# Normalising each head pair inside the scan stage, with the first pair's inverse made one stage earlier

## The chip, the cores and the metric

The kernel runs on one core of a Trainium2 chip. Five engines work side by side, each through its own instructions in program order: TensorE (PE) for matrix products, VectorE (DVE), ScalarE (ACT) and GpSimd (POOL) for work on rows, and SyncE (SP), which here issues most of the DMAs. They meet by semaphores. The metric is the device time of one launch in microseconds (us), lower is better.

## The reference, cut to what matters

The program is two whole network blocks. The change touches one layer of the second, an RWKV-7 mixer with 16 heads of width 64 over 768 positions (512 latent, 256 context), scanned in both directions:

```
r, k, v, z, decays, a, kk = features(h)            # 1024 channels = 16 heads x 64
state_t = state_(t-1) * decay_t + (rank-one corrections from kk, a, k, v)
y_t     = state_t r_t,  forward and backward, summed
y       = (y - mean(y over the head)) * rsqrt(var(y over the head) + 64e-5) * ln_gain + ln_bias
y       = (y + bonus) * gate          # bonus = (sum_head r*kd*r_k) * v, gate from z
x       = x + layer_gate * (y @ w_out)
```

The scan is done in chunks of 64 positions. Each chunk needs the inverse of a unit lower triangular matrix; it is built from the inverses of its 32x32 diagonal blocks, and these come from forward substitution.

## The kernel before

The program is a list of stages. Between stages every compute engine waits until all four have finished the last one (`stage_done`, in `program`, L3126 in the profile is that wait's drain); SP only waits where a stage's `sync` says so. For the RWKV layer the stages are norm, `RwkvFeatures`, `RwkvTerms`, `RwkvScan`, `RwkvOutput` and `Residual`. All but the norm and features work on the eight pairs of heads (KD = 8), 128 channels each, one after the other.

`RwkvTerms` makes, for each pair, five rows of factors per direction and chunk, and the 24 diagonal blocks to be inverted. SP stores them to DRAM (`terms`, `blocks`, `bonus`; L2380 to L2391). POOL multiplies rows (L2414 to L2425), DVE scans, divides and multiplies (L2561 to L2598), ACT does the functions, PE some small products. Its last act on POOL is to wait until everything is stored.

`RwkvScan` takes 24 passes, three per pair (positions 0, 1, 2), each over four chunks in both directions. `make` builds a pass's matrices, and the four sequential state steps of the pass before (`step`) are woven into it. `self.taken` counts passes whose factors were consumed. SP's program for pair m is, in this order:

- `terms(m, 0)` and `terms(m, 1)`: five loads of 256 KB each (L2741), and SP waits for each to land before it issues the next;
- `inverse(m)`: wait until POOL has made the pair's inverses (`inverse_ready`), store them in two layouts (L2751, L2752), wait for both stores to land, and gather them back in 12 small loads (L2760, L2761);
- the load of the next pair's blocks (L2768);
- `terms(m, 2)`.

POOL takes one pair after the other: wait for the blocks, set the diagonal (L2777), 30 steps of substitution, each a product (L2783) and a sum (L2785) on 96 partitions, and a transposed copy (L2787). For the first pair DVE does this at the stage's start instead, before its own work. PE waits for the gathered inverse before the products of L2853; L2805 is the helper that issues all its 64-wide products.

`RwkvOutput` then goes over the pairs again: a matmul with a block of ones gives the mean of each head (L3044), DVE subtracts it (L3077), ACT squares (L3063), a second matmul sums, ACT takes the root (L3067), DVE inverts it (L3083) and multiplies (L3085, L3087), POOL adds the bonus and multiplies by the gate (L3098, L3100), both of which SP loads (L3038). `Residual` needs all eight pairs.

The helper `pairs` (L377 to L383) runs two loop bodies per turn of a hardware loop. Many stages of the program use it, in and outside this layer.

## Time and profile before

| | us |
|---|---|
| three runs | 5809.6 median, 5803.69 to 5816.3 |
| the profiled execution | 5804.21 |
| its span (first to last instruction) | 5801.8 |
| RwkvTerms | about 3236 to 3500 in the span |
| RwkvScan | about 3500 to 4004.5 |
| RwkvOutput | about 4004.5 to 4093 |

A line of the profile gives start or busy time in us. "x15" is a count of instructions. In brackets stands how long the engine had been idle and what ended it. SPq is SP's queue of instructions, of which the profile shows the issue of each DMA, not the time of its transfer.

### The profile page before, as it was taken

How to read it: one execution, taken by the hardware profiler on the slowest of the kernel's cores; microseconds unless marked ns; L12 is line 12 of the kernel's file. 1: busy time of each engine (PE TensorE's matmuls, PEld its weight loads, DVE VectorE, ACT ScalarE, POOL GpSimd, SP SyncE). 2: the span in 40 equal slices, each digit the busy share in tenths (PEclk: the TensorE clock that was granted, in tenths of full speed). 3: DMA queues.
4: the chain of work that ended last, by engine and by line, in shares of the span. 5: the costliest groups of instructions: out<-in, count | busy, mean ns of one | idle time of the engine just before them, and what ended most of it. 6: DMA issues, size and time to landing. Idle time of an engine off the chain costs nothing.

```text
span 5801.8 us, 74255 instructions
## 1 busy us (share of the span) xinstructions
PE 5067.3 (87%) x28334; PEld 2816.2 (49%) x28334; DVE 2134.7 (37%) x3582; ACT 1263.7 (22%) x2161; POOL 650.0 (11%) x831
## 2 busy tenths in 40 slices
PE   6977778899899989998799546997789999999998
PEld 3556635544344434554455326996434444343443
DVE  2347644431133022772400594445324444301110
ACT  2113313320022021110100451222113333211120
POOL 0014300000000000110000353552000000000000
PEclk9988989999999999999899667998889999899999
DMA  3311240022122212442022354342110000022112
GB/s 138 102 61 73 70 152 26 18 80 87 43 80 76 74 39 81 147 151 76 29 89 88 138 205 123 101 103 66 47 47 24 18 18 18 12 82 72 65 69 72
DMA packets 159011, 444.15 MB, mean 77 GB/s; under 512 B 73824, under 2 KB 74080, under 8 KB 141280
## 3 DMA queue, kind: packets, MB, share of 16 engines
q1 hardware_dynamic: 137248, 355.44, 18.3%
q0 software_dynamic: 21568, 85.99, 4.4%
q8 instruction: 137, 2.24, 0.2%
q14 instruction: 58, 0.48, 0.0%
HBM read 372.18 MB, written 69.21 MB: 76 GB/s over the span
## 4 chain that ended last, share of the span: by engine, by line
PE 65%; issue 9%; DVE 7%; DMA 7%; PEld 5%; ACT 2%; DVEq 2%; POOL 1%; SPq 1%; POOLq 1%; PEldq 0%; ACTq 0%
PE psum L373 44%; PE psum L2255 6%; PEld psum L373 5%; DMA sbuf<-terms 3%; PE psum L2805 3%; PE psum L1981 2%; PE psum L1980 2%; PE psum L635 1%; DMA sbuf<-w_side 1%; PE psum L2003 1%; PE psum L1016 1%; DVE sbuf L650 1%; PE psum L1261 1%; DVE sbuf L3083 1%; SPq L2761 1%
## 5 line engine op out<-in xcount | busy, mean ns | idle before, releaser
L373 PE MATMUL psum<-sbuf 128*128 128x512 f32 (+4 forms) x8640 | 3210.3, 532 | 209.0 <-DVEq L1472 61.8
L373 PEld LDWEIGHTS psum<-sbuf 128*128 128x128 f32 (+1 forms) x8640 | 1568.3, 191 | 1816.1 <-issue 1585.0
L2805 PE MATMUL psum<-sbuf 64*64 64x64 f32 (+1 forms) x10752 | 422.9, 238 | 39.7 <-SPq L2743 28.1
L2805 PEld LDWEIGHTS psum<-sbuf 64*64 64x64 f32 x10752 | 411.9, 138 | 46.3 <-issue 33.0
L2255 PE MATMUL psum<-sbuf 128*128 128x512 f32 (+1 forms) x1088 | 356.4, 489 | 32.4 <-DVE sbuf L2235 30.7
L2255 PEld LDWEIGHTS psum<-sbuf 128*128 128x128 f32 x1088 | 206.6, 190 | 182.3 <-issue 163.0
L1478 DVE SCALAR_TENSOR_TENSOR sbuf<-psum,sbuf 128x512 f32 x64 | 42.3, 682 | 660.9 <-PE psum L373 660.9
L585 DVE CUSTOM_DVE_ANT_0 sbuf<-sbuf 128x1024 f32<-128x1024 f32 x160 | 213.1, 1332 | 36.2 <-DMA sbuf<-w_side 16.0
L1698 POOL TENSOR_TENSOR sbuf<-sbuf 128x768 f32<-128x768 f32 (+1 forms) x32 | 45.1, 1410 | 1543.8 <-DVEq L1760 1332.8
L2904 ACT ACTIVATE sbuf<-psum 128x256 f32<-128x256 f32 (+3 forms) x384 | 128.5, 368 | 395.1 <-PE psum L2805 315.3
L2452 PE MATMUL psum<-sbuf 64*128 64x512 f32 (+2 forms) x192 | 90.1, 712 | 133.2 <-POOL sbuf L2422 57.6
L618 ACT ACTIVATE sbuf<-sbuf 128x512 f32<-128x512 f32 (+1 forms) x114 | 52.9, 551 | 670.0 <-DVEq L3126 651.3
L575 POOL DMA_DIRECT2D sbuf<-w_side x128 | 68.5, 535 | 866.6 <-DVE sbuf L585 862.8
L666 DVE TENSOR_SCALAR sbuf<-sbuf 128x512 f32<-128x512 f32 (+1 forms) x68 | 36.3, 533 | 332.5 <-ACT sbuf L1524 189.0
L1748 ACT ACT_TABLE_LOAD x32 | 41.1, 1283 | 491.4 <-PEq L1733 491.4
L2097 DVE TENSOR_REDUCE sbuf<-psum 128x1 f32<-128x768 f32 x64 | 61.3, 957 | 211.3 <-PE psum L1981 211.3
L2452 PEld LDWEIGHTS psum<-sbuf 64*128 64x128 f32 (+1 forms) x192 | 39.8, 263 | 179.4 <-POOL sbuf L2422 63.4
L635 PE MATMUL psum<-sbuf 128*128 128x512 f32 (+1 forms) x228 | 92.4, 563 | 34.1 <-ACT sbuf L618 34.1
L1980 PE MATMUL psum<-sbuf 128*128 128x512 f32 (+1 forms) x256 | 117.3, 541 | 3.5 <-DVE sbuf L2088 3.5
L1981 PE MATMUL psum<-sbuf 64*128 64x512 f32 (+1 forms) x256 | 119.7, 548 | 0.0
L2785 POOL TENSOR_TENSOR sbuf<-sbuf 96x30 f32<-96x30 f32 (+14 forms) x210 | 109.1, 520 | 30.4 <-issue 0.9
L1770 DVE SCALAR_TENSOR_TENSOR sbuf<-psum,sbuf 128x512 f32<-128x512 f32 (+1 forms) x48 | 30.3, 659 | 221.7 <-PEq L1733 217.0
(282 smaller groups left out, 4734.7 us busy)
## 6 DMA issues: line engine op xcount, KB each, us to landing
sbuf<-w_side POOLq DMA_DIRECT2D x128, 512.0 KB, 3.8
sbuf<-w_sgu_uz SPq DMA_DIRECT2D x32, 1088.0 KB, 5.0
sbuf<-terms SPq DMA_DIRECT2D x120, 256.0 KB, 2.7
sbuf<-w_up SPq DMA_DIRECT2D x22, 1024.0 KB, 4.9
sbuf<-w_merge SPq DMA_DIRECT2D x8, 2560.0 KB, 9.0
sbuf<-w_sgu_v SPq DMA_DIRECT2D x8, 2048.0 KB, 8.0
sbuf<-w_sgu_out SPq DMA_DIRECT2D x16, 1024.0 KB, 4.9
terms<-sbuf SPq DMA_DIRECT2D x8, 1920.0 KB, 11.3
```

What stands on the lines that cost most here:

```text
L373: last = nc.tensor.matmul(out, w, x, start=(n == 0), stop=(n == len(pairs) - 1))
L575: pool.dma_start(self.slot[b], src).then_inc(self.landed[b], 16)
L585: last = v.tensor_tensor_reduce(junk, self.slot[b], self.rows[:, c], 1.0, 0.0, ALU.mult, ALU.add, self.sums[:, b, n:n + 1])
L635: last = self.nc.tensor.matmul(self.chip.bank(n, t), self.chip.const("ones"), squares[:, i], start=(i == 0), stop=(i == k - 1))
L1980: t.matmul(s[:, a:a + w], self.qn[u][:, q], self.kn[u][:, a:a + w], start=True, stop=False)
L1981: last = t.matmul(s[:, a:a + w], rot[:, q], self.kr[u][:, a:a + w], start=False, stop=True)
L2097: v.tensor_reduce(self.mx[:, n:n + 1], self.s_bank(n), AX.X, ALU.max)
L2255: last = self.nc.tensor.matmul(self.wide(b)[:, at:at + width], w[:, k], xs[:, k, at:at + width], start=(k == 0), stop=(k == KD - 1))
L2452: last = t.matmul(out[:, at:at + width], w, x[:, at:at + width], start=True, stop=True)
L2785: engine.tensor_tensor(x[:, j + 1:BLK, 0:j], x[:, j + 1:BLK, 0:j], product, ALU.add)
L2805: last = t.matmul(out[hs], lhs[hs], rhs[hs], start=start, stop=stop)
L2904: copy = lambda to, of: a.activation(to, of, ACT.Copy)
```

## The change

Three things change.

First, `RwkvOutput` is gone as a stage. Its work for pair m-1 or m-2 is woven into the scan of pair m: PE's sums into positions 1 and 2, ACT's square and root beside them, DVE's centring behind the third step of position 1, the reciprocal in two halves (positions 2 and then 0), the scaling two pairs later at position 1. POOL adds the bonus and the gate for pair m-3 behind the substitution of pair m (`output`). SP loads bonus and gate for pair m-1 at the end of its turn for pair m, into one buffer each; from the second such load on it first waits until POOL has finished with the buffer (`output_done`).

Second, the first pair's substitution is no longer DVE's. POOL does it in the terms stage, six of the thirty steps behind its own rows of each of the pairs 3 to 7 (counted from 0), and SP stores it there; it also loads the first 1.3 MB of factors and the masks there. The blocks of the terms stage have one buffer in place of two, and POOL at the end of the stage waits for the stores of the even pairs, the first factors and the stored inverse, not for everything.

Third, `pairs` is written out: a Python loop where there was a hardware loop. So are SP's and POOL's loops in the terms stage.

```diff
@@ -378,7 +378,7 @@
 
     if n == 1:
         return body(0, 0)
-    with eng.Fori(0, n // 2) as i:
+    for i in range(n // 2):
         for u in range(2):
             body(i, u)
...
+def substitute(eng, engine, x, products, first, end):
+    x = x.rearrange("p (i c) -> p i c", c=BLK)
+    for j in range(first, end):
+        n = BLK - 1 - j
+        left = x[:, j + 1:BLK, j:j + 1].broadcast_to([4 * NBLK, n, j])
+        right = x[:, j:j + 1, 0:j].broadcast_to([4 * NBLK, n, j])
+        product = products[0:4 * NBLK, 0:n * j].rearrange("p (i c) -> p i c", c=j)
+        engine.tensor_tensor(product, left, right, ALU.mult)
+        eng.drain()
+        engine.tensor_tensor(x[:, j + 1:BLK, 0:j], x[:, j + 1:BLK, 0:j], product, ALU.add)
+        eng.drain()
+
...
+            if m == KD - 1:
+                sp.dma_start(self.chip.view(A_WORK, len(SCAN_MASKS) * CH), d["scan_const"][:, T + BLK:]).then_inc(self.masks_in, 16)
+            sp.dma_start(d["bonus"][m], self.x[u][:, 1]).then_inc(self.bonus_stored[u], 16)
+            if m + 2 < KD:
                 sp.wait_ge(self.bonus_stored[u], 16 * i + 16)
                 load(m + 2, u)
             sp.dma_start(to[:, :, 0].rearrange("b p w -> p b w"), flat[0]).then_inc(self.stored[u], 16)
...
         load(0, 0)
         load(1, 1)
-        with sp.Fori(0, KD // 2 - 1) as i:
-            for u in range(2):
-                store(2 * i + u, u, i, True)
-        for u in range(2):
-            store(KD - 2 + u, u, KD // 2 - 1, False)
+        for m in range(KD):
+            store(m, m % 2, m // 2)
+            if m == 0:
+                sp.wait_ge(self.blocks_stored, 2 * self.BLOCKS_STORED)
+                sp.dma_start(self.inverse, d["blocks"][0]).then_inc(self.first_blocks, 16)
+            if m == KD - 2:
+                sp.wait_ge(self.stored[0], self.STORED * 2)
+                sp.wait_ge(self.bonus_stored[0], 16 * (KD // 2))
+                sp.dma_start(self.scan_terms[0], d["terms"][0].rearrange("p d w -> p (d w)")).then_inc(self.first_terms, 16)
+                sp.wait_ge(self.first_inverse, 1)
+                sp.dma_start(d["inverse"][0, 0], self.inverse).then_inc(self.inverse_stored, 16)
+                sp.dma_start(d["inverse"][0, 1], self.inverse_t).then_inc(self.inverse_stored, 16)
...
-        def step(m, u, i, more):
-            directed(m + 1, 1 - u, i + u)
+
+
+        first(0, 0, 0)
+        for m in range(KD - 1):
+            directed(m + 1, (m + 1) % 2, (m + 1) // 2)
             pool.drain()
-            if more:
-                cut(m + 2, u)
-            weighted(m + 1, 1 - u, i + u)
-
-        self.each(pool, first, step, nothing)
-        for u in range(2):
-            pool.wait_ge(self.stored[u], self.STORED * (KD // 2) + self.STORED)
-            pool.wait_ge(self.bonus_stored[u], 16 * (KD // 2))
-            pool.wait_ge(self.blocks_stored[u], self.BLOCKS_STORED * (KD // 2) + self.BLOCKS_STORED)
+            if m + 2 < KD:
+                cut(m + 2, m % 2)
+            weighted(m + 1, (m + 1) % 2, (m + 1) // 2)
+            if m == 2:
+                pool.wait_ge(self.first_blocks, 16)
+                g.memset(self.inverse[:, 0:BLK * BLK:BLK + 1], 1.0)
+            if m >= 2:
+                substitute(pool, g, self.inverse, self.inverse_products, 6 * (m - 2) + 1, 6 * (m - 1) + 1)
+        g.tensor_copy(*transposed(self.inverse_t, self.inverse))
+        pool.drain().then_inc(self.first_inverse, 1)
+        pool.wait_ge(self.stored[0], self.STORED * (KD // 2) + self.STORED)
+        pool.wait_ge(self.first_terms, 16)
+        pool.wait_ge(self.inverse_stored, 32)
 
     def tensor(self, pe):
         t = self.nc.tensor
...
@@ -2728,29 +2793,31 @@
     INVERSE_IN = 12 * 16
 
     def sync(self, sp):
-        d = self.chip.dram
+        d, b4 = self.chip.dram, self.before
+        sp.wait_ge(b4.first_terms, 16)
+        sp.sem_inc(self.ready, 1)
         sp.wait_ge(self.chip.stage_done, 4 * self.index)
-        sp.dma_start(self.x[0], d["blocks"][0]).then_inc(self.blocks_in[0], 16)
-        sp.dma_start(self.chip.view(self.masks_at, len(SCAN_MASKS) * CH), d["scan_const"][:, T + BLK:]).then_inc(self.masks_in, 16)
 
         def terms(m, b):
             sp.wait_ge(self.taken, 3 * m + b + 1)
+            sp.wait_ge(b4.stored[m % 2], b4.STORED * (m // 2) + 2 * b4.STORED)
             src = d["terms"][3 * m + b].rearrange("p d w -> p (d w)")
             for part in range(PARTS):
                 w = slice(part * LOAD, part * LOAD + LOAD)
-                sp.dma_start(self.terms[:, b, w], src[:, w]).then_inc(self.landed, 16)
-                sp.wait_ge(self.landed, (48 * m + 16 * b) * PARTS + 16 * part + 16)
+                sp.dma_start(self.terms[b][:, w], src[:, w]).then_inc(self.landed, 16)
+                sp.wait_ge(self.landed, (48 * m + 16 * b - 16) * PARTS + 16 * part + 16)
             sp.sem_inc(self.ready, 1)
 
         def inverse(m):
             u = m % 2
             if m == 0:
...
             else:
                 sp.wait_ge(self.inverse_ready, m)
-            sp.dma_start(d["inverse"][m, 0], self.x[u]).then_inc(self.inverse_stored, 16)
-            sp.dma_start(d["inverse"][m, 1], self.xt[u]).then_inc(self.inverse_stored, 16)
-            sp.wait_ge(self.inverse_stored, 32 * m + 32)
+                sp.dma_start(d["inverse"][m, 0], self.x[u]).then_inc(self.inverse_stored, 16)
+                sp.dma_start(d["inverse"][m, 1], self.xt[u]).then_inc(self.inverse_stored, 16)
...
 
+        def blocks(m):
+            sp.wait_ge(b4.blocks_stored, b4.BLOCKS_STORED * m + 2 * b4.BLOCKS_STORED)
+            sp.dma_start(self.x[m % 2], d["blocks"][m]).then_inc(self.blocks_in[m % 2], 16)
+
+        def output(m):
+            if m > 0:
+                sp.wait_ge(self.output_done, m)
+            sp.dma_start(self.bonus, d["bonus"][m]).then_inc(self.output_in, 16)
+            sp.dma_start(self.gate, d["rkvz"][4 * m + 3]).then_inc(self.output_in, 16)
+
+        inverse(0)
+        for u in range(2):
+            sp.wait_ge(b4.bonus_stored[u], 16 * (KD // 2))
+            sp.wait_ge(b4.stored[u], b4.STORED * (KD // 2) + b4.STORED)
         for m in range(KD):
-            terms(m, 0)
+            if m > 0:
+                terms(m, 0)
             terms(m, 1)
-            inverse(m)
+            if m > 0:
+                inverse(m)
             if m + 1 < KD:
-                sp.dma_start(self.x[(m + 1) % 2], d["blocks"][m + 1]).then_inc(self.blocks_in[(m + 1) % 2], 16)
+                blocks(m + 1)
             terms(m, 2)
-
-
...
     def gpsimd(self, pool):
-        self.nc.gpsimd.memset(self.y, 0.0)
+        g = self.nc.gpsimd
+        for u in range(2):
+            pool.wait_ge(self.before.stored[u], self.before.STORED * (KD // 2) + self.before.STORED)
+        g.memset(self.y, 0.0)
         pool.drain().then_inc(self.zeroed, 1)
         products = self.chip.view(A_W + D + 2 * BLK * BLK, BLK * BLK)
+
+        def output(m):
+            y = self.row(m)
+            pool.wait_ge(self.scaled, m + 1)
+            pool.wait_ge(self.output_in, 32 * m + 32)
+            g.tensor_tensor(y, y, self.bonus, ALU.add)
+            pool.drain()
+            g.tensor_tensor(y, y, self.gate, ALU.mult).then_inc(self.output_done, 1)
+
         for m in range(1, KD):
-            self.substitute(pool, self.nc.gpsimd, m, products)
+            x = self.x[m % 2]
+            pool.wait_ge(self.blocks_in[m % 2], 16 * ((m + 1) // 2))
+            g.memset(x[:, 0:BLK * BLK:BLK + 1], 1.0)
+            substitute(pool, g, x, products, 1, BLK - 1)
+            g.tensor_copy(*transposed(self.xt[m % 2], x))
             pool.drain().then_inc(self.inverse_ready, 1)
+            if m >= 3:
+                output(m - 3)
+        for m in range(KD - 3, KD):
+            output(m)
 
     def tensor(self, pe):
...
@@ -2865,8 +2953,16 @@
                         last = t.matmul(self.narrow(d, 2)[self.rows(h, d), s], self.z[d][rows, s], inverse[1][d][rows, s, self.cols(1 - d)], start=True, stop=True)
                         if (s, h) == (BATCH - 1, 1):
                             last.then_inc(self.tt_sums[d], 1)
+            if m > 0 and pos == 1:
+                mean(m - 1)
+            if m > 0 and pos == 2:
+                variance(m - 1)
             if past:
                 step(*past, 3)
+            if m > 0 and pos == 1:
+                wait(self.centred, m)
+            if m > 0 and pos == 2:
+                wait(self.rooted, m)
             for d in range(2):
                 wait(self.tt_out[d], n + 1)
...
                 each(flat(self.slots(d, 0, 2)), lambda s: self.w[d][:, s, 0], flat(self.mb_b[d])).then_inc(self.corrected[d], 1)
+
+        def sums(x):
+            for i in range(2):
+                last = t.matmul(self.row_sum(i), self.chip.const("pair_ones"), x[:, self.row_half(i)], start=True, stop=True)
+            return last
+
+        def mean(m):
+            for d in range(2):
+                wait(self.y_added[d], 3 * m + 4)
+            sums(self.row(m)).then_inc(self.mean_sum, 1)
+
+        def variance(m):
+            wait(self.squared, m + 1)
+            sums(self.squares).then_inc(self.var_sum, 1)
 
         def step(n, m, pos, s):
...
@@ -2955,9 +3083,18 @@
                 lbt = self.slots(d, 0, 2)
                 v.tensor_scalar(self.lbt[d], lbt[:, :, 0, self.cols(1 - d)], -1.0, None, mult).then_inc(self.evacuated[d], 1)
                 v.tensor_tensor(self.mb_b[d][:, :, 0], lbt[:, :, 1], self.mask(before[d] + "_diag"), mult).then_inc(self.evacuated[d], 1)
-            if past:
-                for s in range(BATCH):
+            for s in range(BATCH):
+                if past:
                     step(*past, s)
+                if s == 2 and m > 0 and pos == 1:
+                    centre(m - 1)
+            if m > 0 and pos == 2:
+                dve.wait_ge(self.rooted, m)
+                reciprocal(0)
+            if m > 1 and pos == 0:
+                reciprocal(1)
+            if m > 1 and pos == 1:
+                scale(m - 2)
             for d in range(2):
                 x = self.source(pos, d)
...
 
-        def alone(*past):
-            begin(*past)
+        def centre(m):
+            y = self.row(m)
+            dve.wait_ge(self.mean_sum, m + 1)
+            for i in range(2):
+                half = y[:, self.row_half(i)]
+                last = v.scalar_tensor_tensor(half, self.row_sum(i), -1.0 / RW, half, mult, add)
+            last.then_inc(self.centred, 1)
+
+        def reciprocal(i):
+            half = self.row_half(i)
+            v.reciprocal(self.inv[:, half], self.squares[:, half])
+
+        def scale(m):
+            y = self.row(m)
+            dve.drain()
+            v.tensor_tensor(y, y, self.inv, mult)
+            dve.drain()
+            v.tensor_scalar(y, y, self.chip.vec("ln_gain", m, 1), self.chip.vec("ln_bias", m, 1), mult, add).then_inc(self.scaled, 1)
+
+        def alone(n, m, pos):
+            begin(n, m, pos)
+            reciprocal(1)
             for s in range(BATCH):
-                step(*past, s)
+                step(n, m, pos, s)
+            centre(m)
+            scale(m - 1)
+            dve.wait_ge(self.rooted, m + 1)
+            reciprocal(0)
+            reciprocal(1)
+            scale(m)
         self.passes(make, alone)
-
-class RwkvOutput(Stage):
-
...
-        pairs(pool, KD, body)
 
 
 def rwkv_layer(chip, layer):
     y = chip.view(Y_RWKV, KD, T)
     gate = modulated(chip, layer, 2)
-    return [norm2(chip, layer, True), RwkvFeatures(chip), RwkvTerms(chip), RwkvScan(chip), RwkvOutput(chip),
+    norm, features, terms = norm2(chip, layer, True), RwkvFeatures(chip), RwkvTerms(chip)
+    return [norm, features, terms, RwkvScan(chip, terms),
             Residual(chip, "w_rwkv_out", KD, lambda k: y[:, k, TC:T], gate[0], lambda k: y[:, k, 0:TC], gate[1])]
 
 

```

Here is SP in the scan before, from the load of one pair's blocks on. The names are the DMA's target and source.

```order
L2768 DMA sbuf<-blocks 96x1024
L2741 DMA sbuf<-terms 128x512 x15
L2751 DMA inverse<-sbuf 96x1024
L2752 DMA inverse<-sbuf 96x1024
L2760 DMA sbuf<-inverse 32x12x32
```

And the same stretch after, for pair 3's blocks. Some semaphores show under a name that an earlier stage had given to the same number: `w_mod1_turned` is the landing of the part before, `states_decayed` is `taken`, `states_weighted` is `inverse_ready`.

```order
L2832 DMA sbuf<-blocks 96x1024 [waits terms_blocks_stored]
L2807 DMA sbuf<-terms 128x512 [waits terms_stored0,states_decayed]
L2807 DMA sbuf<-terms 128x512 [waits w_mod1_turned] x4
L2837 DMA sbuf<-bonus 128x768 [waits w_mod1_turned,scan_output_done]
L2838 DMA sbuf<-rkvz 128x768
L2807 DMA sbuf<-terms 128x512 [waits terms_stored1,states_decayed]
L2807 DMA sbuf<-terms 128x512 [waits w_mod1_turned] x4
L2807 DMA sbuf<-terms 128x512 [waits w_mod1_turned,terms_stored1,states_decayed]
L2807 DMA sbuf<-terms 128x512 [waits w_mod1_turned] x4
L2818 DMA inverse<-sbuf 96x1024 [waits w_mod1_turned,states_weighted]
```

The two new loads stand between the factors of position 2 and those of the next pair, and the first of them waits for `scan_output_done`.

POOL in the scan before, from the end of one pair's substitution to the beginning of the next:

```order
L2783 TENSOR_TENSOR sbuf<-sbuf 96x30
L2785 TENSOR_TENSOR sbuf<-sbuf 96x30
L2787 COPY sbuf<-sbuf 96x1024
L2777 MEMSET sbuf 96x32 [waits states_shrunk]
L2783 TENSOR_TENSOR sbuf<-sbuf 96x30
```

And after, from the end of pair 3's substitution on:

```order
L2304 TENSOR_TENSOR sbuf<-sbuf 96x30
L2878 COPY sbuf<-sbuf 96x1024
L2869 TENSOR_TENSOR sbuf<-sbuf 128x768 [waits scan_output_in,scan_scaled]
L2871 TENSOR_TENSOR sbuf<-sbuf 128x768
L2876 MEMSET sbuf 96x32 [waits scan_blocks_in0]
```

The bonus and gate of pair 0 (L2869, L2871) come behind pair 3's inverse; what the second of them signals is the `scan_output_done` of SP's list.

POOL in the terms stage before, over the end of one pair and the start of the next (`ssd_cut` is an older name of the number that ACT signals here):

```order
L2422 TENSOR_TENSOR sbuf<-sbuf 128x768 [waits ssd_cut]
L2425 TENSOR_TENSOR sbuf<-sbuf 128x768 [waits terms_kk_done]
L2425 TENSOR_TENSOR sbuf<-sbuf 128x768
L2411 ISA
L2412 ISA [waits inputs_here]
L2414 TENSOR_TENSOR sbuf<-sbuf 128x768 [waits ssd_cut]
```

And after, where twelve substitution instructions stand between the two (here those of the first such turn, the middle ones left out):

```order
L2459 TENSOR_TENSOR sbuf<-sbuf 128x768 x2
L2479 MEMSET sbuf 96x32
L2302 TENSOR_TENSOR sbuf<-sbuf 96x30
L2304 TENSOR_TENSOR sbuf<-sbuf 96x30
L2302 TENSOR_TENSOR sbuf<-sbuf 96x58
L2304 TENSOR_TENSOR sbuf<-sbuf 96x29x2
...
L2304 TENSOR_TENSOR sbuf<-sbuf 96x25x6
L2448 TENSOR_TENSOR sbuf<-sbuf 128x768 x2
```

POOL's rows of the next pair (L2448, before L2414) are now queued behind the substitution.

## Rows read from the trace of the kernel before

**Rows 1.** The page's first line and its table of the engines.
```profile
span 5801.8 us, 74255 instructions
PE 5067.3 (87%) x28334; PEld 2816.2 (49%) x28334; DVE 2134.7 (37%) x3582; ACT 1263.7 (22%) x2161; POOL 650.0 (11%) x831
```
**Rows 2.** Busy us by stage (terms, scan, output): PE, PEld, DVE, ACT, POOL, PEclk, DMA.
```profile
3236.00:3500.00 264.00, 110.78 (x1728) 59.88 (x1728) 217.12 (x144) 142.93 (x177) 114.27 (x56) 0.58 0.56 197
3500.00:4004.50 504.50, 441.48 (x12288) 430.50 (x12288) 224.57 (x656) 128.46 (x384) 230.25 (x435) 0.93 0.36 94
4004.50:4093.00 88.50, 34.21 (x64) 16.18 (x64) 59.85 (x32) 20.49 (x22) 28.84 (x16) 0.64 0.25 83
```
**Rows 3.** Timeline of SP's queue, one turn: start, us, what.
```profile
3660.43 0.47 SPq L2768 DMA_DIRECT2D sbuf<-blocks  x1
3660.94 42.94 SPq L2741 DMA_DIRECT2D sbuf<-terms  x15
3706.24 0.34 SPq L2751 DMA_DIRECT2D inverse<-sbuf  x1
...
3710.94 0.32 SPq L2760 DMA_DIRECT2D sbuf<-inverse  x1
...
3718.98 0.47 SPq L2768 DMA_DIRECT2D sbuf<-blocks  x1
```
**Rows 4.** Timeline of POOL in the same turn.
```profile
3664.40 0.15 POOL L2777 MEMSET sbuf<- 96x32 f32 x1 [18.63 <-DMA sbuf<-blocks]
3703.10 1.96 POOL L2787 COPY sbuf<-sbuf 96x1024 f32<-96x1024 f32 x1
```
**Rows 5.** Chain of waits: PE's first product behind each gather (pairs 1, 7).
```profile
3602.94 0.54 PE psum L2853 x32
3951.30 0.65 PE psum L2853 x32
```
**Rows 6.** Output stage, chain of waits: first pair.
```profile
4004.52 2.86 PE psum L3044 x8
...
4012.95 4.95 DVE sbuf L3083
```
**Rows 7.** POOL's additions of the bonus in that stage: ns min/median/max, first and last start.
```profile
L3098 POOL TENSOR_TENSOR sbuf<-sbuf x8: 1802/1807/1812, 4020.3 to 4089.3; 128x768 f32 x8
```
**Rows 8.** Terms stage, a pair's turn: POOL and DVE side by side.
```profile
3352.46 3.59 POOL L2425 TENSOR_TENSOR sbuf<-sbuf 128x768 f32<-128x768 f32 x2 [4.30 <-DVE sbuf L2576]
3354.87 1.99 DVE L2584 TENSOR_TENSOR sbuf<-sbuf 128x768 f32<-128x768 f32 x1
3359.63 0.95 DVE L2584 TENSOR_TENSOR sbuf<-sbuf 128x768 f32<-128x768 f32 x1
```
**Rows 9.** POOL's substitution in the scan, by line.
```profile
L2785 POOL TENSOR_TENSOR sbuf<-sbuf 96x30 f32<-96x30 f32 (+14 forms) x210 | 109.1, 520 | 30.4 <-issue 0.9
L2783 POOL TENSOR_TENSOR sbuf<-sbuf 96x30 f32<-96x30 f32 (+14 forms) x210 | 101.7, 484 | 29.2 <-issue 0.4
```
**Rows 10.** The last pair of the terms stage, and the scan's start.
```profile
3472.13 4.29 POOL L2425 TENSOR_TENSOR sbuf<-sbuf 128x768 f32<-128x768 f32 x2 [6.79 <-DVE sbuf L2576]
3484.08 0.44 SPq L2384 DMA_DIRECT2D terms<-sbuf  x1
3484.56 4.34 SPq L2386 DMA_DIRECT2D terms<-sbuf  x3
3490.69 6.79 SPq L2391 DMA_DIRECT2D blocks<-sbuf  x4
3541.44 0.47 SPq L2768 DMA_DIRECT2D sbuf<-blocks  x1
```
**Rows 11.** A loop through `pairs` that PE drains (first gated unit): three bodies.
```profile
2292.54 0.97 PEld L1724 LDWEIGHTS psum<-sbuf 128*128 128x128 f32 x8 [0.70 <-issue]
2315.66 0.97 PEld L1724 LDWEIGHTS psum<-sbuf 128*128 128x128 f32 x8 [1.22 <-issue]
2338.26 0.97 PEld L1724 LDWEIGHTS psum<-sbuf 128*128 128x128 f32 x8 [0.70 <-issue]
```

More of the change, by code:

```diff
@@ L2309, in __init__ @@
         self.x = [chip.view(at + u * 4 * T, 4, T) for u in range(2)]
+        self.scan_terms = [chip.view(at + u * 4 * T, 2 * BATCH * TERMS * CH) for u in range(2)]
         at += 8 * T
@@ L2369, in load, with store @@
         def load(m, u):
[L2370 to L2375 removed]
+            sp.dma_start(self.x[u], d["rkvz"][4 * m:4 * m + 4].rearrange("c p w -> p c w")).then_inc(self.loaded[u], 16)
+        def store(m, u, i):
+            to = d["terms"][3 * m:3 * m + 3]
             width = BATCH * TERMS * CH
@@ L2651, in __init__ @@
         at += 2 * NBLK * CH
+        row = lambda: chip.view(at, T)
+        self.bonus, at = row(), at + T
+        self.gate, at = row(), at + T
+        self.squares, at = row(), at + T
+        self.inv, at = row(), at + T
         assert at <= A_END, at
@@ L2769, in sync @@
             terms(m, 2)
[L2773 to L2787 removed]
+            if m > 0:
+                output(m - 1)
@@ L2898, in alone @@
                 step(*past, s)
+            mean(KD - 1)
+            variance(KD - 1)
         self.passes(make, alone)
```

182 lines of the change are left out of this document (56 added, 126 removed).

## The prediction

> **What bounds the kernel now.** I read the page's head first: a span of 5801.8 us for a profiled execution of 5804.2, so 2.4 us lie around the span [rows 1]. PE is busy for 87% of it, but the change touches three stages only, so I went on to the busy times by stage [rows 2]. The terms stage takes 264 us and DVE is busy for 217 of them. The scan takes 504.5 us and PE is busy for 441 of them. The output stage takes 88.5 us and no engine is near full: DVE has 60, PE 34. That stage is what the change takes away as a stage.
>
> The scan looks bound by PE, and it nearly is. But PE's first product behind each gathered inverse comes at 3602.94 for pair 1 and at 3951.30 for pair 7 [rows 5]: (3951.30 - 3602.94) / 6 = 58.06 us per pair, and PE's work in it is about 441 / 8 = 55. What sets the 58 is found in SP's queue. One turn goes from the load of one pair's blocks at 3660.43 to the next at 3718.98, 58.55 us [rows 3]. In it: 15 parts of factors, each awaited, from 3660.94 to 3706.24 (45.3 us, 3.02 each); the two stores of the inverse and the wait for them, to 3710.94 (4.7 us); twelve gathers, to 3718.98 (8.0 us). The reader should see that SP stands still at each wait and nothing behind it is issued: between the stores at 3706.24 and the first gather at 3710.94 no factor is loaded, though position 2's are next but thirteen. Beside this runs POOL's turn [rows 4]: blocks in at 3664.40 (3.97 us behind the load's issue), copy done at 3703.10 + 1.96 = 3705.06, so 40.66 us of substitution. POOL ends 1.2 us before SP wants to store. Two chains of the same length, side by side: this is what the change disturbs.
>
> **SP's new wait, the large term.** At the end of its turn for pair m, SP loads bonus and gate for pair m-1 and waits first until POOL has used those of pair m-2. POOL does that behind the substitution of pair m+1, whose blocks SP has loaded only one group of five parts earlier. So SP issues those blocks, loads position 2 (15.1 us), and stands until the whole substitution is over. Queued behind it are the ten parts of the next pair's positions 0 and 1; behind those, the storing and gathering of the inverse that has long been ready; behind that, the next blocks, for which POOL waits. The two chains that ran side by side become one in a row:
>
> - load of the blocks until POOL starts, 3.97 [rows 3, 4]
> - substitution and copy, 40.66 [rows 4]
> - bonus and gate on POOL, two at 1.81 and the drain between, 3.9 [rows 7]
> - SP wakes and issues two loads, 1.0
> - ten parts at 3.02, 30.2 [rows 3]
> - stores of the inverse and their wait, 4.7 [rows 3]
> - twelve gathers, 8.0 [rows 3]
>
> The sum is 92.4 us against 58.06, so 34.4 more. It strikes whenever the wait is there and the substitution it leans on is in the future: the turns for pairs 2 to 6, five of them, which delay the inverses of pairs 3 to 7. In pair 1's turn there is no wait, in pair 7's POOL has no more substitution. 5 x 34.4 = +172. Bounds: the parts could take 2.7 each with the queues otherwise quiet, or 3.4 beside the 786 KB of bonus and gate, which makes 89 to 96 per turn, +155 to +190. Nothing else in the turn hides it: PE has 55 us of work per pair and will stand for some 37.
>
> What the issue order means can be put by a rule. The rows above show SP silent for 4.7 us while it waits for a store. The Trainium skill, "DMA: Bandwidth & Descriptors", Anatomy of one DMA, says that DMA engines do not themselves wait on semaphores; the issuing sequencer does, before dispatch. By that rule a wait in front of one load holds all that follow on that sequencer, and the sum is as above; if only the awaited load were held, the turn would be the old one plus two issues, and the total that of the second rival below. By that rule, the trace agrees.
>
> **Pair 1's turn.** Bonus and gate of pair 0 are loaded without a wait. SP's chain of 58.55 is the longer of the two by 1.2, so it grows by the two issues, 0.7, and a share of the queues for 786 KB, in all +3 (0 to 5).
>
> **The terms stage and the scan's start.** POOL now has twelve substitution instructions (and once the copy) behind its rows of pairs 3 to 7. POOL has 114 us in 264, so the time is there. But POOL and DVE do not run freely side by side [rows 8]: DVE's L2584 takes 0.95 us alone and 1.99 when it starts at 3354.87 while POOL's L2425 runs until 3352.46 + 3.59 = 3356.05. It waits for POOL's instruction to end and then takes its 0.9. Substitution takes 0.50 us per instruction (210.8 us for 420) [rows 9]. It begins where DVE has its eight multiplications L2584 to L2589, and each may wait for one: 8 x 0.5 = 4 us per pair, five pairs, 20 us, of which 17 fall before the last pair's rows. DVE sets this stage's pace, so I take them in full; below, nothing is lost if DVE always comes first; above, twice as much, if POOL's delay reaches PE's sums too.
>
> That is the first place where a rule bears. The Trainium skill, "SBUF — State Buffer", Who interferes with whom, has it that a DVE instruction with two SBUF inputs and a GpSimd instruction that reads SBUF exclude each other for the whole instruction. By it the 4 us per pair stand; with shared bandwidth and instructions of half a microsecond the loss would be less than half. By that rule, the row agrees, 1.99 against 0.95.
>
> Then the end of the stage [rows 10]. POOL's last rows end at 3476.42 + 17 = 3493.4. The last twelve instructions (small ones: 4.2 us, gaps 1.8) alternate with eight of DVE's (6.4), then the copy 2: 3507.8. SP stands before the stores of this inverse (0.8), and pair 7's stores are behind it: 4.8 for the factors (3484.08 to 3488.90) and 6.8 for the blocks (L2391), so SP is free at 3520. The stage ends near 3513, not at 3491 where DVE ends now. The gathers of pair 0 take 8.0, the five parts of position 1 take 15.1, and the blocks of pair 1 go out at 3543.5 to 3544.5. Now they go out at 3541.44 [rows 10]. So DVE's 25 us of substitution and the wait for the last stores vanish, and PE begins some 10 us earlier, but it then waits for pair 1's inverse as late as before: +3. Bounds: -23 without any of DVE's delay, +20 with twice as much.
>
> **The last pair and the tail.** Behind pair 7's gather, PE now also sums for pair 6, twice 2.86 [rows 6], waits at each for DVE or ACT (about 2 each), and DVE's half reciprocals (4.95 / 2 each) stand before rows for which PE waits: +12 (5 to 20). For pairs 1 to 6 this lies in PE's idle 37 us. After the last step come pair 7's mean, square, variance and root (8.4 us, 4004.52 to 4012.95), the reciprocal and the scaling, until POOL starts 15.8 us in (4020.3) [rows 6, 7]. With pair 6's scaling before it (1.8), POOL's two rows (3.9) and the end, 22. The stage of 88.5 goes [rows 2]: 22 - 88.5 = -66.5.
>
> **The loops written out.** In the gated units PE drains at each body, and a body behind the loop's turn starts later: periods of 23.12 and 22.60 alternate [rows 11], 0.5 per turn of the loop, 8 turns in each of two stages: -7. Elsewhere PE's queue runs ahead of the loop. Bounds -20 (as much again in the others) and +5, if straight code is fetched late.
>
> **The sum.** 172 + 3 + 3 + 12 - 66.5 - 7 = +116.5 on the profiled 5804.2, 5920.7. The median of the runs shown is 5.4 higher; I say 5922.
>
> **The rivals.**
> 1. The start is gained after all: POOL's substitution slips between DVE's rows, and pair 1's blocks go out 26 us earlier than I have it. Half of POOL's time in that stage is free, which speaks for it; rows 8 speak against. 5922 - 26 = 5896.
> 2. Faster: SP's wait is over when SP comes to it. The mechanism is the same wait with POOL's bonus and gate done within 15.1 us of the load of the blocks. Then the turn is 61 us and all is 5922 - 5 x 31 = 5767. It decides at (66.5 + 7 - 3 - 3 - 12) / 5 = 11: as long as a turn costs less than 11 us more than now, the removed stage pays for it. Against it: POOL's list has these two instructions behind the substitution of 40.66 us.
> 3. The standstill of 37 us per pair costs PE its clock. In the scan 0.93 is granted, in the output stage with its gaps 0.64 [rows 2]. If pair 7's passes run slower by a quarter, and the terms stage stretches by double: 5922 + 14 + 17 = 5953.
>
> **Chances.** My forecast 0.73, rival 1 0.12, rival 3 0.08, rival 2 0.06, something between that ends at no change 0.01. Two runs of this kernel can be told apart from about 0.2%, 12 us. Faster 0.06, same 0.01, slower 0.93. The range takes in rivals 1 and 3 and both bounds of the large term partly: 5873 to 5960.
>
> **What would show it.** In SP's queue a wait of some 33 us (3.97 + 40.66 + 3.9 less the 15.1 of position 2) on POOL's gate multiplication before the loads of bonus, five times; turns of 89 to 96 us for pairs 3 to 7 and near 61 for pair 2; PE waiting for factors and for the inverse some 35 us per pair; POOL idle for about 48 us per turn. In the terms stage the eight multiplications of DVE are longer beside POOL, by 0.5 on the mean. I am wrong if SP does not wait there, or if the turns stay near 60.

## The result and the profile after

The changed kernel takes 5881.66 us (median of 4 runs, 5874.13 to 5886.56) against 5812.95 for the kernel before: a ratio of 1.0116, interval 1.0098 to 1.0134. That is 69 us slower, where 112 were forecast (5922 against the 5809.6 shown before). The two profiled executions differ by 5876.6 - 5801.8 = 74.8 us in span, and this is the number that the traces can account for.

The head of the page after, to be held against [rows 1]:

```profile
span 5876.6 us, 72492 instructions
PE 5068.6 (86%) x28334; PEld 2822.2 (48%) x28334; DVE 2112.9 (36%) x3536; ACT 1243.2 (21%) x2152; POOL 713.1 (12%) x893
```

The same work is done in more time. By stage (terms stage, then scan with the normalisation in it; columns as in [rows 2]):

```profile
3232.00:3505.00 273.00, 105.22 (x1728) 56.44 (x1728) 225.35 (x146) 142.74 (x176) 174.14 (x118) 0.61 0.56 199
3505.00:4174.60 669.60, 476.67 (x12352) 450.68 (x12352) 258.50 (x640) 143.69 (x409) 263.60 (x451) 0.85 0.29 79
```

The scan went from 504.5 to some 670 us, which is more than the scan and the output stage together had. PE is busy in 71% of it, before in 88%.

SP's queue in one turn after, from the load of pair 4's blocks to that of pair 5's, answers to [rows 3]:

```profile
3734.51 0.47 SPq L2832 DMA_DIRECT2D sbuf<-blocks  x1
3735.08 11.99 SPq L2807 DMA_DIRECT2D sbuf<-terms  x5
3783.81 0.32 SPq L2837 DMA_DIRECT2D sbuf<-bonus  x1
3784.18 0.43 SPq L2838 DMA_DIRECT2D sbuf<-rkvz  x1
3784.71 26.44 SPq L2807 DMA_DIRECT2D sbuf<-terms  x10
3813.53 0.32 SPq L2818 DMA_DIRECT2D inverse<-sbuf  x1
...
3817.91 0.32 SPq L2827 DMA_DIRECT2D sbuf<-inverse  x1
...
3823.91 0.47 SPq L2832 DMA_DIRECT2D sbuf<-blocks  x1
```

POOL in the same turn answers to [rows 4]:

```profile
3738.11 0.15 POOL L2876 MEMSET sbuf<- 96x32 f32 x1 [43.91 <-DMA sbuf<-blocks]
3777.77 2.00 POOL L2878 COPY sbuf<-sbuf 96x1024 f32<-96x1024 f32 x1
3780.01 1.82 POOL L2869 TENSOR_TENSOR sbuf<-sbuf 128x768 f32<-128x768 f32 x1 [0.24 <-issue]
3781.97 1.82 POOL L2871 TENSOR_TENSOR sbuf<-sbuf 128x768 f32<-128x768 f32 x1
```

Read the two together. SP has issued position 2's last part near 3747 and then nothing until 3783.81, which is where POOL's gate multiplication ends (3781.97 + 1.82 = 3783.79). Only then come the loads, the ten parts, the stores of an inverse that was finished 34 us before, the gathers, and the next blocks, for which POOL in its turn has waited for 44 us. The queue's waits over the whole span and PE's between 3600 and 4100 say the same (total, times, longest):

```profile
SPq L2837 <- POOL sbuf L2871: 221.6, 7, 35.1
SPq L2827 <- DMA inverse<-sbuf: 24.3, 7, 3.6
```

```profile
PE psum L2893 <- SPq L2809: 77.4, 5, 16.4
PE psum L2941 <- DMA sbuf<-inverse: 76.8, 5, 16.6
```

Five of SP's seven waits on POOL stand in the turns of pairs 2 to 6 and make 168.5 us, 33.7 each; the other two come at the end, where POOL has no substitution left. PE waits in each of five turns once for factors (L2893, the helper's products) and once for the inverse, 31 us together. Its first product behind a gather, for pairs 2, 3 and 7, answers to [rows 5]:

```profile
3646.83 0.45 PE L2941 MATMUL psum<-sbuf 32*32 32x32 f32 x32
3736.24 0.65 PE L2941 MATMUL psum<-sbuf 32*32 32x32 f32 x32 [15.52 <-DMA sbuf<-inverse]
4098.07 0.65 PE L2941 MATMUL psum<-sbuf 32*32 32x32 f32 x32 [15.67 <-DMA sbuf<-inverse]
```

(4098.07 - 3646.83) / 5 = 90.25 us per turn, against 58.06.

The end of the scan answers to [rows 6, 7]:

```profile
4157.92 1.53 PE L2977 MATMUL psum<-sbuf 128*128 128x384 f32 x4 [1.19 <-DVE sbuf L3130]
4161.44 1.56 PE L2977 MATMUL psum<-sbuf 128*128 128x384 f32 x4 [1.99 <-ACT sbuf L3047]
4163.94 4.96 DVE L3143 RECIPROCAL sbuf<-sbuf 128x384 f32<-128x384 f32 x2 [1.62 <-ACT sbuf L3052]
4170.78 1.80 POOL L2869 TENSOR_TENSOR sbuf<-sbuf 128x768 f32<-128x768 f32 x1 [4.62 <-DVE sbuf L3150]
4172.72 1.80 POOL L2871 TENSOR_TENSOR sbuf<-sbuf 128x768 f32<-128x768 f32 x1
4175.00 1.22 PE L373 MATMUL psum<-sbuf 128*128 128x512 f32 x1 [12.00 <-DVEq L1472]
```

The kernel before has this at the start of its output stage, for the first two pairs at once:

```profile
4004.52 2.85 PE L3044 MATMUL psum<-sbuf 128*128 128x512 f32 x8 [1.25 <-DVEq L3126]
4006.11 0.96 DVE L3077 SCALAR_TENSOR_TENSOR sbuf<-psum,sbuf 128x768 f32<-128x768 f32 x1 [1.80 <-PE psum L3044]
4008.66 1.28 ACT L3063 ACT_TABLE_LOAD   x1 [0.71 <-DVE sbuf L3077]
4010.81 1.28 ACT L3067 ACT_TABLE_LOAD   x1
```

What was a stage of 88.5 us is a tail of 17 (4157.8 to 4175.0).

With events that both traces have, the 74.8 us split as follows. Each line is how much later or earlier the event comes after, and the change since the event before it.

| event | before | after | difference | since the last |
|---|---|---|---|---|
| DVE's first row of the terms stage | 3245.4 | 3241.4 | -4.0 | -4.0 |
| DVE's last row of pair 7 there ends | 3483.6 | 3486.7 | +3.1 | +7.1 |
| blocks of pair 1 issued | 3541.4 | 3528.6 | -12.8 | -15.9 |
| blocks of pair 2 issued | 3600.5 | 3585.1 | -15.4 | -2.6 |
| blocks of pair 3 issued | 3660.4 | 3644.2 | -16.2 | -0.8 |
| PE's first product on pair 7's inverse | 3951.3 | 4098.1 | +146.8 | +163.0 |
| DVE's last sum of the scan ends | 4004.3 | 4157.8 | +153.5 | +6.7 |
| first matmul of the residual stage | 4093.55 | 4175.00 | +81.4 | -72.0 |
| end | 5801.8 | 5876.6 | +74.8 | -6.6 |

The first line is no more than scatter: in the traces of this kernel and of its variants below, which have the same instructions ahead of the terms stage, DVE's first row there starts between 3238.0 and 3248.0.

### The profile page after: what moved, and what is told of

It is laid out like the page before. It is cut to its first block, busy times and chain, and to the rows that moved or that the text cites. A ratio compares the mean times of both kernels' runs of the same rounds, so it can differ in the third digit from the quotient of the medians.

```text
span 5876.6 us, 72492 instructions
## 1 busy us (share of the span) xinstructions
PE 5068.6 (86%) x28334; PEld 2822.2 (48%) x28334; DVE 2112.9 (36%) x3536; ACT 1243.2 (21%) x2152; POOL 713.1 (12%) x893
## 4 chain that ended last, share of the span: by engine, by line
PE 61%; issue 13%; POOLq 6%; DVE 6%; PEld 5%; DMA 2%; ACT 2%; POOL 2%; DVEq 2%; PEldq 0%; SPq 0%; ACTq 0%
PE psum L373 43%; PE psum L2255 6%; PEld psum L373 5%; POOLq L2305 2%; POOLq L2303 2%; PE psum L1981 2%; PE psum L1980 2%; PE psum L635 1%; PE psum L2003 1%; DMA sbuf<-w_side 1%; PE psum L1016 1%; DVE psum L585 1%; DVE sbuf L650 1%; PE psum L1261 1%; DVE sbuf L1375 1%
## 5 line engine op out<-in xcount | busy, mean ns | idle before, releaser
L2893 PE MATMUL psum<-sbuf 64*64 64x64 f32 (+1 forms) x10752 | 434.0, 241 | 103.4 <-SPq L2809 81.1
L2893 PEld LDWEIGHTS psum<-sbuf 64*64 64x64 f32 x10752 | 421.0, 141 | 119.0 <-SPq L2809 82.6
L2255 PE MATMUL psum<-sbuf 128*128 128x512 f32 (+1 forms) x1088 | 357.9, 490 | 30.1 <-DVE sbuf L2235 29.1
L2255 PEld LDWEIGHTS psum<-sbuf 128*128 128x128 f32 x1088 | 207.3, 191 | 180.8 <-issue 163.0
L2493 PE MATMUL psum<-sbuf 64*128 64x512 f32 (+2 forms) x192 | 86.4, 675 | 145.5 <-ACT sbuf L2567 63.6
L2304 POOL TENSOR_TENSOR sbuf<-sbuf 96x30 f32<-96x30 f32 (+14 forms) x240 | 140.5, 585 | 34.8 <-issue 1.1
L2097 DVE TENSOR_REDUCE sbuf<-psum 128x1 f32<-128x768 f32 x64 | 61.3, 958 | 211.3 <-PE psum L1981 211.3
L2302 POOL TENSOR_TENSOR sbuf<-sbuf 96x30 f32<-96x30 f32 (+14 forms) x240 | 133.0, 554 | 33.4 <-issue 1.5
L3123 DVE TENSOR_SCALAR sbuf<-psum,sbuf 128x64 f32<-128x64 f32 x192 | 45.7, 280 | 226.7 <-PE psum L2893 225.4
L1748 ACT ACTIVATE sbuf<-psum 128x512 f32<-128x512 f32 (+1 forms) x48 | 23.5, 525 | 479.4 <-PEq L1733 479.4
L635 PE MATMUL psum<-sbuf 128*128 128x512 f32 (+1 forms) x228 | 91.6, 559 | 34.2 <-ACT sbuf L618 34.2
```

What stands on the lines that cost most here:

```text
L635: last = self.nc.tensor.matmul(self.chip.bank(n, t), self.chip.const("ones"), squares[:, i], start=(i == 0), stop=(i == k - 1))
L2255: last = self.nc.tensor.matmul(self.wide(b)[:, at:at + width], w[:, k], xs[:, k, at:at + width], start=(k == 0), stop=(k == KD - 1))
L2302: engine.tensor_tensor(product, left, right, ALU.mult)
L2304: engine.tensor_tensor(x[:, j + 1:BLK, 0:j], x[:, j + 1:BLK, 0:j], product, ALU.add)
L2493: last = t.matmul(out[:, at:at + width], w, x[:, at:at + width], start=True, stop=True)
L2893: last = t.matmul(out[hs], lhs[hs], rhs[hs], start=start, stop=stop)
```

## The experiments

My theory was the forecast's: SP's loads of bonus and gate wait for POOL at a place where everything that the next pair needs is queued behind them. The rivals: the loads' own bytes, POOL's two further rows, or the sums woven into PE's passes cost the time.

**Loads behind the gathers.** A few lines of SP's order:

```diff
             if m > 0:
                 inverse(m)
+            if m > 1:
+                output(m - 2)
             if m + 1 < KD:
                 blocks(m + 1)
             terms(m, 2)
-            if m > 0:
-                output(m - 1)
+        output(KD - 2)
         output(KD - 1)
```

> SP's loads of bonus and gate (for pair m-2 now) stand behind the gathers of pair m and ahead of the next blocks; POOL has used the buffer by then, so SP should not stand. If the order in SP's queue is the cause: turns of 59.5 us in place of 90.25, five times, so 5881.7 - 154 = 5728 (5715 to 5745). If it is the 786 KB per pair, or POOL's two more rows, or the sums woven into PE's passes, those are all still there and the time stays within 20 us of 5882.

Measured: 5736.98 us (5732.36 to 5740.14), ratio to the kernel before 0.9849 (0.9833 to 0.9866). Between pair 1 and pair 7, SP's waits were these:

```profile
SPq L2807 <- DMA sbuf<-terms: 196.7, 69, 5.4
SPq L2809 <- DMA sbuf<-terms: 44.1, 18, 3.0
SPq L2827 <- DMA inverse<-sbuf: 25.0, 6, 5.4
SPq L2818 <- POOLq L2880: 2.4, 3, 1.6
```

No wait for POOL's gate is left in the steady turns. The turn is 61.3 us ((3898.34 - 3530.55) / 6 between issues of the blocks), not the 59.5 expected. The blocks are now issued behind the two loads and land later: in the turn from 3650.75 POOL starts 5.8 us behind their issue, where it was 3.6, and SP waits for POOL's inverse three times, if briefly. Every byte, row and sum of the change is still there, so against the 58.06 of the kernel before the rivals together are worth at most 3.2 us per turn, where the changed kernel lost 32. The change's 1.2% loss is a 1.5% gain once the order is other.

**The wait put earlier still.**

```diff
-            terms(m, 2)
             if m > 0:
                 output(m - 1)
+            terms(m, 2)
```

> The same waiting load is put ahead of the factors of position 2, so that these five parts are queued behind it too. By the theory of one chain in a row the turn grows by what no longer runs beside the substitution, 13 to 15 us, five times: turns of 104 us and 5882 + 70 = 5952. By the rival, that bytes or POOL's rows cost, nothing moves: 5882.

Measured: 5976.24 us (5956.08 to 5983.01), ratio 1.0251 (1.0226 to 1.0276). SP's wait got longer by what it no longer covers:

```profile
SPq L2837 <- POOL sbuf L2871: 243.2, 5, 48.8
```

Five waits of 48.6 us in place of some 34. PE's first products on the inverses of pairs 2 and 7 come at 3660.93 and 4184.82, 104.8 us per turn; 104 were expected. So the sum of a chain in a row predicts the turn in both cases. The whole time it misses: 5952 were expected, 24 us less than was measured. The profiled execution is 104.7 us longer than that of the changed kernel, of which the five turns are 72.7. Another 20.6 come behind pair 7's first product (97.5 us to the first matmul of the residual stage, before this edit 76.9): here too the factors of position 2 are now queued behind a wait on POOL, and PE waits 16.9 us for them. The expectation had counted five turns and left this one out. The rest, about 11, lies mostly ahead of pair 2's products, where this execution was late from the start (DVE's first row of the terms stage at 3248.0, in the changed kernel 3241.4).

**POOL issues the loads itself**, behind its own gate multiplication; SP has neither loads nor wait.

```diff
...
+        def fetch(m):
+            if m > 0:
+                pool.wait_ge(self.output_done, m)
+            pool.dma_start(self.bonus, self.chip.dram["bonus"][m]).then_inc(self.output_in, 16)
+            pool.dma_start(self.gate, self.chip.dram["rkvz"][4 * m + 3]).then_inc(self.output_in, 16)
...
             if m >= 3:
                 output(m - 3)
+                fetch(m - 2)
...
```

> POOL issues the loads of bonus and gate itself, behind its own gate multiplication; SP has no such load and no such wait. Same bytes, same rows on POOL. By the theory turns of 58 to 60 us and 5730 (5715 to 5750), POOL's issues of some 0.5 us each being hidden behind its signal that the inverse is ready. By the rivals as in the first run, near 5882.

Measured: 5736.17 us (5727.77 to 5741.02), ratio 0.9853 (0.9837 to 0.9870), turns of 59.6 us where 58 to 60 were expected. The same wait on the same signal is now in a queue that has nothing urgent behind it, and it costs nothing that shows. From the first run this is not told apart in time.

**No substitution in the terms stage.**

```diff
-                substitute(pool, g, self.inverse, self.inverse_products, 6 * (m - 2) + 1, 6 * (m - 1) + 1)
+                pass
```

> Leaves out the first pair's substitution (its inverse is then not computed); everything else as in the changed kernel. If POOL's substitution rows are what made DVE's eight multiplications longer, these fall from about 1.3 back to about 1.05 us mean and the terms stage gets some 7 us shorter. If the longer stage had another cause (the single buffer of blocks, the unrolled queues), it keeps its 245 us from DVE's first to last row.

Measured, in one execution only: a span of 5869.3 us, and DVE's first to last row of the stage takes 3478.1 + 0.95 - 3241.1 = 238.0 us, against 245.3 in the changed kernel and 238.2 before. So the substitution is what costs 7.3 us there. But not in the way that was expected: DVE's eight multiplications per pair (L2625 to L2630, 64 rows) have a mean of 1.17 us without it and 1.23 with it, not 1.05 and 1.3. DVE's rows by line and shape, first without, then with the substitution (count, busy us, mean ns, idle before):

```profile
L2605 DVE TENSOR_TENSOR_SCAN sbuf<-sbuf 128x768 f32<-128x768 f32 x16 | 39.2, 2453 | 0.0
L2625 DVE TENSOR_TENSOR sbuf<-sbuf 128x768 f32<-128x768 f32 x16 | 21.0, 1311 | 0.7 <-ACT sbuf L2583 0.7
L2608 DVE TENSOR_TENSOR sbuf<-sbuf 128x768 f32<-128x768 f32 x8 | 17.4, 2176 | 0.6
L2639 DVE TENSOR_TENSOR sbuf<-psum,sbuf 128x768 f32<-128x768 f32 x8 | 7.7, 959 | 12.4 <-PE psum L2534 12.2 <-issue 0.2
```

```profile
L2605 DVE TENSOR_TENSOR_SCAN sbuf<-sbuf 128x768 f32<-128x768 f32 x16 | 38.2, 2391 | 0.0
L2625 DVE TENSOR_TENSOR sbuf<-sbuf 128x768 f32<-128x768 f32 x16 | 22.2, 1387 | 0.7 <-ACT sbuf L2583 0.7
L2608 DVE TENSOR_TENSOR sbuf<-sbuf 128x768 f32<-128x768 f32 x8 | 13.6, 1699 | 0.6
L2639 DVE TENSOR_TENSOR sbuf<-psum,sbuf 128x768 f32<-128x768 f32 x8 | 7.7, 959 | 18.2 <-PE psum L2534 18.2
```

The multiplications L2625 and its like get longer, but L2608 gets shorter, from 2176 to 1699 ns: DVE waits there for a short row of the substitution where it had waited for a long row of POOL's own. Over all its rows with two SBUF inputs DVE is busy for 169.1 us with the substitution and 167.6 without. What remains, 5.8 us, is L2639's longer wait for PE's sums; PE for its part waits in the stage 63.1 us for POOL's L2456 in place of 58.0, and 63.6 for ACT in place of 58.2. That the one wait comes from the other is argued from these sums and was not tested by a run. POOL pays more than DVE: its 60 rows of substitution take 58.4 us here, 0.97 each, against 0.50 in the scan [rows 9].

**The loops written out, alone**, on the kernel before.

```diff
-    with eng.Fori(0, n // 2) as i:
+    for i in range(n // 2):
```

> The kernel before with nothing but the helper's loop written out. By the traces the changed kernel gains 4.0 us ahead of the terms stage and 6.65 behind the scan, and nothing else of the change lies there: 10.6 us less than before, ratio 0.998. If these 10 us were scatter between executions, no difference.

Measured: 5793.63 us (5784.89 to 5804.81), ratio 0.9957 (0.9940 to 0.9973), which is 16 to 35 us less; the profiled span is 14.2 us shorter (5787.6). It is a gain, and larger than the 10.6 expected. The two measures don't agree well. The trace of the kernel before is of one of its fastest executions (5804.2 us, where its runs beside this one took 5811.4 to 5835.6), which may be why; the size is known only as some 14 to 35. In the gated units the bodies that started 23.12 and 22.60 us apart in turn [rows 11] now start 22.51 apart:

```profile
2292.58 0.97 PEld L1724 LDWEIGHTS psum<-sbuf 128*128 128x128 f32 x8 [0.61 <-issue]
2315.09 0.97 PEld L1724 LDWEIGHTS psum<-sbuf 128*128 128x128 f32 x8 [0.61 <-issue]
2337.60 0.97 PEld L1724 LDWEIGHTS psum<-sbuf 128*128 128x128 f32 x8 [0.61 <-issue]
```

From first body to last that is 4.6 us in the first unit and 4.1 in the second, 8.7 of the trace's 14.2.

**The first inverse alone**, with the loops: the changed kernel with the output stage put back and every mean, square, root and scaling taken out of the scan.

```diff
-            if m > 0:
-                output(m - 1)
-        output(KD - 1)
...
-    return [norm, features, terms, RwkvScan(chip, terms),
+    return [norm, features, terms, RwkvScan(chip, terms), RwkvOutput(chip),
...
```

> The changed kernel with the output stage put back and nothing of it in the scan: the loops written out and the first pair's inverse in the terms stage are what is left of the change. By the traces up to pair 1's blocks (7.4 lost in the terms stage, 15.9 and 2.6 gained behind it) this part is worth -11, so with the loops about 22 us under the kernel before, ratio 0.996. By my forecast of this part (+3) only the loops' 7 to 10 would be left. If the scan's start were worth its whole 26 us (pair 0 begins that much earlier), 36 under.

Measured: 5787.63 us (5785.57 to 5790.25), ratio 0.9941 (0.9926 to 0.9956). That is 26 to 43 us under the kernel before. Taken alone it would fit the expectation's third case (36, the whole start gained) and not the 22 or the 7 to 10. But the run above, with the loops alone, was timed beside it and is already 16 to 35 us under; the intervals overlap, the 6 us between the two medians are not told apart from nothing, and this trace is 1.0 us longer than that one. Their traces show why it is little. PE's first product on pair 0's inverse comes at 3515.6 against 3535.6, 20 us earlier, but the last sum of the scan starts at 3997.1 against 3997.8. Most of what pair 0 gains is given back at pair 1, whose blocks are issued at 3529.1 against 3532.7. My expectation from one trace (-11 for this part) was too much; most of the -15.9 in the table is not kept or not this part's.

The three parts then stand like this: loops about -14 to -35, first inverse not told apart from nothing, and the normalisation in the scan +1.8% with its wait (1.0116 / 0.9941) or -0.9% without it (0.9849 / 0.9941), that is +102 or -54 us (by the spans of the traces +88 or -50).

**The next blocks ahead of the inverse**, on top of POOL's own loads.

```diff
-            if m > 0:
-                inverse(m)
             if m + 1 < KD:
                 blocks(m + 1)
+            if m > 0:
+                inverse(m)
```

> POOL issues bonus and gate, and SP loads the next pair's blocks ahead of the stores and gathers of the inverse, so that POOL's substitution no longer waits for them. If POOL's chain still sets the turn (3.97 + 40.66 + 4.7 + 8.0 = 57.3), it drops to some 50 and SP's own chain of 58 remains: 1 to 2 us per turn, 5726 to 5733 against 5736. If SP's fifteen awaited parts set it alone, no change.

Measured: 5743.71 us (5728.83 to 5753.55), ratio 0.9863 (0.9841 to 0.9884): no gain over the 0.9853 of the run without this edit, and the turn is 60.8 us. SP no longer waits for POOL at all. Between 3600 and 4000 it waits 245.2 us for parts, 26.6 for the stores of the inverse and, five times, 20.5 together until a pass was taken (`taken`, signalled behind DVE's L3111). So SP's own chain sets the turn, as the second half of the expectation had it, with a share of those waits in it.

**Two parts in flight**, on top of that: two semaphores in turn, and SP waits for the part before the last.

```diff
...
-                sp.dma_start(self.terms[b][:, w], src[:, w]).then_inc(self.landed, 16)
-                sp.wait_ge(self.landed, (48 * m + 16 * b - 16) * PARTS + 16 * part + 16)
+                k = (3 * m + b - 1) * PARTS + part
+                sp.dma_start(self.terms[b][:, w], src[:, w]).then_inc(self.landing[k % 2], 16)
+                for j in ([k - 1] if part > 0 else []) + ([k] if part + 1 == PARTS else []):
+                    sp.wait_ge(self.landing[j % 2], 16 * (j // 2) + 16)
```

> As the run before, and two parts of factors are in flight at a time. SP's 45 us of parts fall to some 30, so neither SP nor POOL sets the turn; PE's own work does, some 57.5 us with its two new sums: 5736 less 7 turns of 2.5, 5718. If the gathers get slower in fuller queues and PE still waits for them, 5730 or more.

Measured: 5712.13 us (5708.75 to 5715.39), ratio 0.9812 (0.9794 to 0.9830), the fastest of all and 32 us under the run before it, beside which it was timed; 5718 were expected. The blocks go out every 55.4 us, less than the 57.5 that the expectation gave PE. SP and PE between 3600 and 3990:

```profile
SPq L2809 <- DMA sbuf<-terms: 81.6, 53, 3.9
SPq L2809 <- DVEq L3114: 80.7, 11, 11.9
```

```profile
PE psum L2898 <- issue: 3.7, 6, 1.3
PE psum L2946 <- issue: 2.8, 3, 1.4
PE psum L2898 <- DVE sbuf L3128: 2.4, 2, 2.1
PE psum L2946 <- DMA sbuf<-inverse: 1.5, 2, 1.2
```

SP now waits for passes to be taken (the signal after L3114, DVE's), and PE hardly waits for anything: it is busy for 339.9 of the 350 us from 3600 to 3950, so here PE bounds the stage.

## Why the prediction was right

**The mechanism** was right, and it carries the result: SP's wait on POOL turns two chains side by side into one in a row, in the turns of pairs 2 to 6. The trace shows the wait on the instruction named, and moving that one load, to either side or to another queue, moved the time by -145, +95 and -145 us between medians (-138, +105 and -150.5 between traces).

**The turn** was put at 92.4 us and was 90.25 on the mean. Its pieces, in the turn shown, which took 89.4: blocks to POOL 3.60, substitution and copy 41.66 (40.66 forecast), bonus and gate 4.0, the two loads 0.9, ten parts 28.8 (30.2 forecast, now 2.88 each; why they are faster was not tested), stores 4.4, gathers 6.0 (8.0 forecast). Five turns gave +163 where +172 stood. Of the signs that the forecast named, SP's wait (33 us, found 33.7), PE's (35, found 31), POOL's idle time (48, found 44) and pair 2's turn (near 61, found 59.1) came; DVE's multiplications longer by 0.5 us on the mean did not (0.06, see the run without the substitution).

**Pair 1's turn**: +3 forecast, -0.8 found, just outside its bounds of 0 to 5. The two loads cost nothing that shows where nothing waits for them.

**The terms stage and the scan's start**: +3 forecast, 7.1 - 15.9 - 2.6 = -11.4 in the two traces. The step that failed is the one that charged 20 us to DVE's waits behind POOL's substitution; 7.3 were found, and only 1.5 of them in DVE's own rows. The two engines do hold each other up, but I charged only the added waits and not those that the same rows displace. POOL's own rows for the last pair end at 3477.4 and not at 3493.4, 4 us of this because the stage began earlier; its copy ends at 3489.8 and not at 3507.8, and pair 1's blocks go out at 3528.6 and not at 3544. The conclusion that an earlier pair 0 is of no use while pair 1 has to wait held: with this part alone the scan ends within 1 us of where it ends without it (3997.1 and 3997.8).

**The last pair**: +12 forecast, +6.7 found. The text's own pieces add up to more than 12: two sums of 2.86, two waits of about 2 and two half reciprocals of 2.5 are 14.7. And the 2.86 was misread. That row has eight matmul instructions, which are the sums of two pairs, as the rows shown above say: DVE centres the first pair at 4006.11, 1.6 us in. One pair's sum has four and takes 1.56 us after, so two of them cost 3.1 and not 5.7. PE does not wait at them in pair 7's passes; before the last steps it waits 2.1 us behind a half reciprocal. **The tail**: -66.5 forecast, -72.0 found. From the first sum to the root's end it takes 6.0 us where 8.4 were taken over from the output stage, in which two pairs' sums and squares came first and ACT loaded tables twice, 1.28 us each; in the tail there is one pair and no table load. And pair 6's scaling (4160.60) lies beside ACT's square and costs nothing.

**The loops**: -7 forecast, -10.6 between the traces, of which the 4.0 ahead of the terms stage are within scatter; 14 to 35 less in the run that measures them alone. I had counted only the gated units.

All six terms were off on the slow side, by 9, 4, 14, 5, 5.5 and 4 us: 42 together, which is the whole distance from +116.5 to +74.8. No error was set off by another, and 5881.66 lies only 9 us above the lower end of the range. All but pair 1's turn stayed within the bounds that the text had set. The total is also off by a slip: 5920.7 and 5.4 are 5926, not 5922.

**The rivals.** The first (the start is gained after all) held in part in the trace (pair 1's blocks went out 15 us earlier than forecast, not 26), and not to the end of the scan. The second (SP's wait is over when SP comes to it) did not happen, but the first experiment built it: a turn of 61.3 us where the text had 61, and 5737 where it had worked out 5767, for the other five terms were 33 us too slow. The third (PE's clock): over 3600 to 4100 PE was granted 0.84 of its full clock, before the change 0.96 over 3600 to 3950. That is a loss of clock, but PE was not what was waited for there. In pair 7's passes, where it was, 0.92 was granted from 4115 to 4158, and 1.00 in the kernel before from 3968 to 4004, and these passes with the sums in them took 6.7 us more than before, not the 12 and another 14 that the rival needs.

## What to carry to other kernels

A wait in a queue of DMAs is priced by what stands behind it and not by what it guards. Before a load that must wait for a consumer is put in, list what the queue issues next and who waits for that; then put the load where its condition is already met, or in a queue with nothing urgent behind it. And a stage saved (here 72 us) does not show what moving its work cost: the same work was worth -54 us in one order and +102 in another, a few lines apart.

Work that makes one item earlier at the front of a pipeline is worth little if the second item is nearly as late as before: here pair 0 came 20 us earlier, and the end of the scan less than 1.

Before a row's duration is used as a price, count its instructions: the 2.86 us were two sums, not one.

## What the runs showed that was not expected

- Sixty substitution rows on POOL, in a stage where DVE is busy for 217 of 264 us, cost DVE's rows only 1.5 us. Rows of 0.5 us put ahead of POOL's rows of 1.8 us lengthened some of DVE's rows (L2625, 1311 to 1387 ns mean) and shortened others (L2608, 2176 to 1699 ns). POOL's added rows themselves nearly doubled, to 0.97 us each.
- The hardware loops of the helper `pairs` cost the kernel before 16 to 35 us by the timed runs and 14 by the trace, of which 8.7 lie in the gated units. Where the rest lies was not settled.
- Awaiting each 256 KB part costs more than it seems to: with two in flight the turn fell from 60.8 to 55.4 us, though the blocks-first order alone had gained nothing.
